# Dense groups cut into contraction steps over the mixers' slots, earlier rounding of weights, and 16 modulation units moved beside layer 0's feed-forward

## The reference, cut to what matters

```python
for layer in range(2):
    mod_l = adaln_params(c, w_mod[layer], b_mod[layer])        # silu(c) @ w_mod + b_mod, six vectors of 1024
    mod_c = adaln_params(c_ctx, w_mod[layer], b_mod[layer])
    p_l = modulate(x,   norm1_g, mod_l[0], mod_l[1]) @ w_in    # modulate: rmsnorm(x, g) * (1 + scale) + shift
    p_c = modulate(ctx, norm1_g, mod_c[0], mod_c[1]) @ w_in
    a = diff_attention(p[0:3]); b = hgrn2_mixer(p[3:8]); n = neighbourhood_attention(p[8:11]); w = window_gqa(p[11:14])
    x = x + mod_l[2] * (concat(a, b, n, w) @ w_out)
    x = x + mod_l[5] * (square(relu(modulate(x, norm2_g, mod_l[3], mod_l[4]) @ w_ff1)) @ w_ff2)
    # layer 0 does the last two lines for ctx too; layer 1 for x alone
```

## Time and profile before

| what | value |
|---|---|
| median of 3 runs | 2527.3 us (2523.86, 2527.3, 2529.58) |
| profiled execution, its own time | 2523.21 us |
| its span, first to last instruction | 2521.4 us |
| TensorE busy | 2078.6 us (82%) |
| VectorE, ScalarE, GpSimd busy | 1159.5, 766.8, 610.0 us |
| mean granted TensorE clock | 0.908 |
| loads of 1 MB of `w_ff` and `w_mod`, issue to landing, median | 5.3 us |
| GpSimd's `wlo` of one unit (L637), mean | 4.6 us |
| chain that ended last | TensorE 67%, VectorE 17%, ScalarE 9% |

### The profile page before, as it was taken

The page is one execution under the profiler, slowest core; times in us unless marked ns, Lnnn a source line. Parts: engine busy times, 40 slices in busy tenths (PEclk is TensorE's granted clock), DMA queues, the critical chain, the costliest instruction groups (busy, mean ns, idle before and its releaser), DMA issues.

```text
span 2521.4 us, 29860 instructions
## 1 busy us (share of the span) xinstructions
PE 2078.6 (82%) x12484; PEld 1705.4 (68%) x12484; DVE 1159.5 (46%) x1782; ACT 766.8 (30%) x1225; POOL 610.0 (24%) x263
## 2 busy tenths in 40 slices
PE   5779786687775698999999997879688639899998
PEld 3667564466664586888888885658477536688887
DVE  2544536555499715222221316454685884522322
ACT  2522222223333325222221315232344432522321
POOL 0121010001166122222222221301001552344432
PEclk9889797778898798999999998989799778999999
DMA  7312020323165011122112212111001011232231
GB/s 261 59 51 84 1 67 1 101 88 80 42 204 193 5 51 49 52 67 67 57 62 67 68 50 39 55 33 34 17 18 51 0 34 51 67 100 88 96 100 67
DMA packets 178918, 168.86 MB, mean 67 GB/s; under 512 B 29200, under 2 KB 176096, under 8 KB 178656
## 3 DMA queue, kind: packets, MB, share of 16 engines
q1 hardware_dynamic: 176704, 161.18, 20.9%
q10 hardware_dynamic: 2080, 5.77, 0.8%
HBM read 159.07 MB, written 2.10 MB: 64 GB/s over the span
## 4 chain that ended last, share of the span: by engine, by line
PE 67%; DVE 17%; ACT 9%; issue 4%; POOL 2%; DMA 1%; ACTq 0%; SPq 0%; DVEq 0%; POOLq 0%
PE gp L691 53%; PE sp L823 3%; PE gp L858 2%; ACT DA_p L1184 2%; POOL HGx_kd L613 2%; PE sp L734 1%; PE tp L838 1%; ACT nt L1097 1%; PE sp L814 1%; PE gp L712 1%; DVE small L1578 1%; DVE sp L1453 1%; PE sp L921 1%; DVE sp L1452 1%; DMA raw<-in_w_mod 1%
## 5 line engine op out<-in xcount | busy, mean ns | idle before, releaser
L637 POOL TENSOR_TENSOR wlo<-raw,whi 128x2048 fp32r<-128x2048 f32 x98 | 452.4, 4617 | 1684.3 <-ACT whi L1079 1684.1
L691 PE MATMUL gp<-xhi,whi 128*128 128x512 f32 (+1 forms) x1584 | 584.1, 369 | 114.5 <-DVE xlo L1473 53.0
L691 PE MATMUL gp<-xlo,whi 128*128 128x512 f32 (+1 forms) x1584 | 570.8, 360 | 0.0
L691 PE MATMUL gp<-xhi,wlo 128*128 128x512 f32 (+1 forms) x1584 | 569.3, 359 | 0.0
L691 PEld LDWEIGHTS gp<-xhi,whi 128*128 128x128 f32 x1584 | 312.1, 197 | 170.2 <-issue 55.8
L691 PEld LDWEIGHTS gp<-xlo,whi 128*128 128x128 f32 x1584 | 311.7, 197 | 43.0 <-issue 1.7
L691 PEld LDWEIGHTS gp<-xhi,wlo 128*128 128x128 f32 x1584 | 310.8, 196 | 43.2
L1079 ACT ACTIVATE whi<-raw 128x2048 fp32r<-128x2048 f32 x98 | 186.8, 1908 | 426.3 <-PE gp L691 425.2
L1833 DVE SCALAR_TENSOR_TENSOR xT<-gp,mods,xT 128x512 f32<-128x512 f32 x120 | 78.6, 662 | 475.9 <-PE gp L691 475.9
L691 PE MATMUL gp<-hhi,whi 128*128 128x512 f32 (+1 forms) x768 | 273.7, 356 | 9.3 <-ACT frel L1393 6.3
L691 PE MATMUL gp<-hlo,whi 128*128 128x512 f32 (+1 forms) x768 | 272.1, 354 | 0.0
(11 more groups left out here) (304 smaller groups left out, 2864.3 us busy)
## 6 DMA issues: line engine op xcount, KB each, us to landing
raw<-in_w_ff SPq DMA_DIRECT2D x64, 1024.0 KB, 5.3
raw<-in_w_mod SPq DMA_DIRECT2D x48, 1024.0 KB, 5.3
raw<-in_w_in SPq DMA_DIRECT2D x20, 1024.0 KB, 5.1
raw<-in_w_in SPq DMA_DIRECT2D x24, 256.0 KB, 4.3
raw<-in_w_out SPq DMA_DIRECT2D x8, 768.0 KB, 4.7
bias<-e SPq DMA_DIRECT2D x96, 32.0 KB
xin<-in_x ACTq DMA_DIRECT2D x1, 2048.0 KB, 9.2
raw<-in_w_out SPq DMA_DIRECT2D x16, 128.0 KB, 4.7
```

Source lines behind the costliest of these rows:

```text
L637: nc.gpsimd.tensor_tensor(wlo[:, s % 2, :, :], raw[:, index[splits[s]] % 2, :, :], whi[:, s % 2, :, :].bitcast(F32), ALU.subtract).then_in ...
L691: mm = pe.matmul(out, lhs, rhs, start=(i == 0 and j == 0), stop=(i == KT - 1 and j == 2))
```

## The change: what it does

1. The plan of the slots (`fill_plan`) spreads a mixer's work by its weight (a step of a 512-token group counts 2, of any other group 1, a row 4/8) evenly over its slots, and may cut a dense group between two contraction steps. The bank stays occupied from one slot to the next.
2. Modulation units in layer 0: none in NA and SW, 14 in DA, 10 in HG, and the last 16 (layer 1's j = 2 to 5) beside layer 0's feed-forward: a row after one unit, its turn after the next, so that each second feed-forward unit has a modulation unit behind it in the load order.
3. `after_unit` emits a rounding once the `whi` slot is free and, if the raw slot was a modulation unit's, that one's row has been passed; the condition on unit i-2 for dense units is gone.
4. On VectorE in the attention mixers, all groups that end in a slot but the last are read ahead of `finish(n + 1)`; the last stays behind it. `ENDS` lists the groups that end in each slot.
5. The norm at the start of a layer waits for that layer's j = 0 and 1 alone.

```diff
+    counts = {("NA", 0): 0, ("SW", 0): 0, ("DA", 0): 14, ("HG", 0): 10, ("NA", 1): 0, ("SW", 1): 0, ("DA", 1): 0, ("HG", 1): 0}
...
+            work = []
+            put = 0
+            for i, (u, c) in enumerate(chunks):
+                work.append((u, c, 2 if c[0] != "tok" and c[1] == 0 else 1))
+                closing = i + 1 < len(chunks) and chunks[i + 1][0] != u
+                while not closing and put < len(units) * (i + 1) // len(chunks):
+                    work.append((units[put], "row", 3))
+                    put += 1
+            work += [(u, "row", 3) for u in units[put:]]
+            total = sum(8 * w if c != "row" else 4 for _, c, w in work)
+            slots = [[] for _ in range(n + 1)]
+            s, done, turn = 0, 0, None
+            for u, c, w in work:
+                if c == "row":
+                    if turn:
+                        slots[s].append(turn)
+                    slots[s].append((u, "row", 0, KT))
+                    turn = (u, "turn", 0, KT)
+                    done += 4
+                    s = min(max(s + 1, done * n // total), n)
+                    continue
+                if turn:
+                    slots[s].append(turn)
+                    turn = None
+                k0 = 0
+                for k in range(KT):
+                    done += w
+                    if done * n >= (s + 1) * total and k < KT - 1:
+                        slots[s].append((u, c, k0, k + 1))
+                        k0 = k + 1
+                        s = min(s + 1, n - 1)
+                slots[s].append((u, c, k0, KT))
...
+            spots = [(0, q, kind, j) for q in range(4) for kind in ("ff1", "ff2") for j in range(4)]
+            for i, u in enumerate(mods):
+                plan["FF"][spots[2 * i]].append((u, "row"))
+                plan["FF"][spots[2 * i + 1]].append((u, "turn"))
...
+ENDS = {key: [[(u, c) for u, c, _, b in slot if b == KT] for slot in slots] for key, slots in FILL.items()}
...
-            def dense(u, *cs, ready=None):
+            def dense(u, *cs, ready=None, part=range(KT)):
...
-                for i, k in enumerate(MIX_ORDER if u[0] == "out" else range(KT)):
+                for i in part:
+                    k = MIX_ORDER[i] if u[0] == "out" else i
...
             def after_unit(u):
-                reached[0] = max(reached[0], index[u])
+                reached[0] = max(reached[0], last_group(u))
...
-                    if index[v] - 2 > reached[0]:
+                    before = units[index[v] - 2]
+                    if before[0] == "mod" and last_group(before) > reached[0]:
                         return
-                    before = units[index[v] - 2] if index[v] >= 2 else None
-                    if before and before[0] == "mod" and last_group(before) > last_group(u):
-                        return
-                    if s >= 2 and last_group(splits[s - 2]) > last_group(u):
+                    if s >= 2 and last_group(splits[s - 2]) > reached[0]:
                         return
...
+                    fill(ENDS[m, l][n][:-1])
                     finish(n + 1)
-                    fill(FILL[m, l][n])
+                    fill(ENDS[m, l][n][-1:])
                     output(n)
...
+                        for w, c in beside(l, q, "ff1", j):
+                            modulation(w, c)
...
+                        for w, c in beside(l, q, "ff2", j):
+                            modulation(w, c)
```

More of the change, by code:

```diff
@@ L139, in fill_plan @@
         tiles = 6 if l < DEPTH - 1 else 4
[L140 to L155, removed]
-            plan[m, l] = slots
@@ L157, in fill_plan @@
-    assert not mods
+        for m, names, n in (("NA", ("SWq", "SWkv"), 2 * tiles), ("SW", ("DAq", "DAk", "DAv"), 2 * tiles),
+                            ("DA", ("HGq", "HGi"), 4 * tiles), ("HG", (), 6 * tiles)):
+            chunks = [(("prj", l, name), c) for name in names for c in chunks_of(("prj", l, name))]
+            units = [mods.pop(0) for _ in range(counts[m, l])]
+            work = []
[30 more added lines that the diff above has]
+                slots[s].append((u, c, k0, KT))
+                if 10 * done * n >= (10 * s + 6) * total:
+                    s = min(s + 1, n - 1)
+            if turn:
+                slots[s].append(turn)
+            plan[m, l] = slots
@@ L179, in dense_order @@
         for m in ("NA", "SW", "DA"):
-            groups.extend((u, c, one) for slot in FILL[m, l] for u, c in slot)
+            groups.extend((u, c, one) for slot in FILL[m, l] for u, c, a, _ in slot if a == 0)
         for n in ("HGf0", "HGf1", "HGg"):
             whole(("prj", l, n))
-        groups.extend((u, c, both) for slot in FILL["HG", l] for u, c in slot)
+        groups.extend((u, c, both) for slot in FILL["HG", l] for u, c, a, _ in slot if a == 0)
         for j in range(4):
@@ L189, in dense_order @@
                     whole((kind, l, q, j))
+                    groups.extend((u, c, both) for u, c in beside(l, q, kind, j))
     return groups
@@ L721, in fill @@
             def fill(slot):
-                for u, c in slot:
+                for u, c, a, b in slot:
                     if u[0] == "mod":
@@ L1283, in hgrn @@
                         if idx >= 4:
-                            fill(FILL["HG", l][idx - 4])
+                            fill(ENDS["HG", l][idx - 4])
                         idx += 1
                 read_out(ntile - 1)
-                for slot in FILL["HG", l][-5:]:
+                for slot in ENDS["HG", l][-5:]:
                     fill(slot)
@@ L1366, in _ @@
                     if before:
-                        fill(FILL[before, l][-2])
-                        fill(FILL[before, l][-1])
+                        fill(ENDS[before, l][-2])
+                        fill(ENDS[before, l][-1])
                     attention(m, l)
@@ L1918, in _ @@
                              .then_inc(ls(l, "h_split"), 1)
+                        fill(beside(l, q, "ff1", j))
                     for j in range(4):
                         add_back(("ff2", l, q, j), 5, l)
+                        fill(beside(l, q, "ff2", j))
                     wait_read(dve, ("ff2", l, q, 3))
```

36 lines of the change are left out of this document (23 added, 13 removed).

## The result

The changed kernel takes 2553.1 us (median of 4 runs, 2543.1 to 2557.2) against 2528.1 for the kernel before in the same comparison (2523.9 to 2529.6): ratio 1.0096, 95% interval 1.0072 to 1.012. It is slower by 25 us, where +7 was forecast. The profiled execution took 2552.55 us (span 2550.7).

| stretch | before | after | change | forecast |
|---|---|---|---|---|
| start to the first NA transposes | 161.6 | 169.5 | +8.0 | +0.9 |
| NA slots, layer 0 | 83.3 | 67.0 | -16.3 | -14.9 |
| SW slots, layer 0 | 105.7 | 88.3 | -17.4 | -15 |
| end of SW's slots to DA's first | 47.3 | 50.9 | +3.6 | 0 |
| DA slots, layer 0 | 176.5 | 157.6 | -18.9 | -16 |

The account below looks back on a forecast made before the run. TensorE was taken to bound NA, SW and feed-forward, VectorE HG, and waits for VectorE's reads to idle TensorE in layer 0's DA. Terms -14 - 15 - 16 + 11.5 - 2 + 35 + 7.5 = +7 gave 2534 us, range 2509 to 2556.

Parts of the forecast that it names:

- its rivals: Whole kernel: DA's clock comes back, 2516, chance 0.28; end of DA covered, 2522, 0.13; feed-forward loses clock, about 2570, 0.08.
- three signs of being wrong: DA's slots under 150 us, feed-forward under 575, or HGf0's first read no later after DA's last slot than before.
- The end of DA: Behind layer 0's DA: HGf0's and HGf1's loads wait for the last modulation rows, roundings precede the squares; +11.5 us.
- Feed-forward, +35: Layer 0's feed-forward: 16 units 24.5, four turn reads +4.2, slow stretches +5, landing waits +1, banks +0.8; +35 us.
- SWkv's rounding ... +0.9: Ahead of layer 0's NA: SWkv's 1.9 us rounding now precedes the copies of NA's values; +0.9 us (0 to 1.9).
- twelve units fewer: -3.5: Layer 0's HG: each unit costs VectorE at most 0.42 + 0.15 us, reads partly overlap; -3.5 us.
- Layer 1, +7.5: Layer 1: cut groups bring late reads, DA +3.2, HGf1's rounding +1.3, NA +3, SW 0; +7.5 us (0 to 13).
- DA, -16: Layer 0's DA slots: shorter waits, early waits, units, pieces, clock and longer loop sum to -16 us (0 to -35).
- 21.6 less 9: Layer 0's DA: earlier reads of turns save 21.6 us of waits, new early waits in ten slots cost 9.
- 20 us that a slot by slot sum leaves unexplained: Layer 0's DA: 20 us unexplained by a slot by slot sum at full clock, of which 6 are taken back.
- The rival that the clock comes back: Layer 0's DA: clock rises from 0.77 to 0.92 to 0.95, DA gives 34 instead of 16, total 2516; chance 0.28.
- The clock term: Layer 0's DA: fewer long waits return clock, -6 us; by the Trainium skill's rule it would be near 0.

Follow-up runs that it names:

- run 4: Changed kernel, with GpSimd's low part of SWq waiting for VectorE's four NA low parts and SWkv rounded behind the copies of NA's values: 2543.9 us, ratio 1.0067.
- run 2: Changed kernel, with layer 0's DA units placed so the last two rows stand in slots 20 and 21: 2542.6 us, ratio 1.0059.
- run 11: Changed kernel with 12 DA and 28 HG units, early read before pieces, both edits ahead of NA, DA's last roundings behind its norm: 2458.1 us, ratio 0.972.
- run 1: Changed kernel, with the 16 modulation units beside layer 0's feed-forward put back into layer 0's HG slots (26 there): 2506.8 us, ratio 0.9917.
- run 3: Changed kernel, with VectorE reading a slot's last group ahead of finish too where a further piece follows: 2517.6 us, ratio 0.9969.
- run 6: Changed kernel, with every read of a slot's groups behind finish, as in the kernel before: 2605.5 us, ratio 1.0314.
- run 8: Changed kernel with the kernel before's unit counts (4 NA, 2 SW, 12 DA, 22 HG, none beside the feed-forward): 2504.0 us, ratio 0.9907.
- run 5: Changed kernel with feed-forward units back in HG, DA's last rows earlier, early read before pieces, and two edits ahead of NA: 2471.9 us, ratio 0.9777.
- run 7: Kernel before, with one edit alone: all groups in a slot but the last are read ahead of finish: 2482.5 us, ratio 0.9823.
- run 9: The kernel with all four edits (2471.9 us), with 12 units in DA, 28 in HG, and DA's roundings two slots later on ScalarE: 2469.1 us, ratio 0.9769.

## Why the forecast came out as it did

**Right in direction and in most of its chain of causes, too low by 18 to 22 us.** The 2553 us measured lie inside the range given (2509 to 2556), but outside the forecast's own (2522 to 2546): the range held by the room that it left for its rivals, none of which came true. "Slower" stood at 0.49, so the direction was half luck. Five stretches were 4 to 7 us longer than written, and the largest error the other way was 2.9. None of the three signs of being wrong showed: the DA slots took 157.6 us (150.7 in run 4, at the edge of the 150 named), the feed-forward 578.2, the first read of HGf0 came 14 us later.

No wait for `mods` is left in NA and SW, none for `wlo` in SW; four waits of 3.9 us in DA and three long ones in layer 1's DA (two for HG_v, together 7.8, one of 4.1 for HG_q) are where the argument put them; two roundings stand ahead of the squares and end 15.2 us behind the last transposes, where 13.4 was written. The end of DA was sized at +11.5 and measured +14.1, and runs 2 and 11 show 10 us of it caused by the squares behind roundings whose loads the last rows gate.

**Feed-forward, +35 against +39.7.** Idle time rose from 4.9 to 13.3 us; 7.1 of the 13.3 are the four turn reads. The clock's share was smaller than the +5 written: two slow stretches, not three. TensorE's busy time rose by 31.3 (run 1's 533.58 to 564.88) where 24.5 of instructions and 3.4 of clock were due; the last 3.4 stay open. The forecast missed one thing beside it: the units shift GpSimd's low parts against VectorE's squares of 128x512, which take 1144 ns in the mean instead of 861. Whether that cost TensorE anything is not shown.

**Start of NA, +0.9 against +8.0.** The step "SWkv's rounding ... +0.9" counted what the rounding does on its own engine. Some 4 us were the collision, which no instruction of the change makes and which several runs of the same program text escape.

**HG, -2 against +3.1.** The step "twelve units fewer: -3.5" failed. With 10 units the levels took 102.6 to 107.7 us in six profiles at clocks of 0.80 to 0.88, with 22 101.2 to 104.6 at 0.90 to 0.94, with 26 104.7 and 104.4 at 0.95 and 0.96, with 28 106.7 and 109.5 at 0.98 and 0.95. VectorE's saved reads are real (95.5 to 92.4 us busy), but its idle time grew by twice as much (5.7 to 11.9 us). Of that growth 2.7 us are waits for a row that TensorE had not finished, shown in the section on the result. The lower clock, with TensorE's scores as a link of the chain, may be the rest: that is read from these rows, no run changed the clock alone, and the 28 units at 0.98 and 0.95 show that the clock does not settle it. The cause stays open.

**Behind SW, 0 against +3.6; the same between layer 1's mixers.** The forecast stopped at the last transposes. The new plan fills the last slot with more groups (two of 3.1 us where one stood), and the product with the values, which the next head norms wait for, is behind them. No run tested this.

**Layer 1, +7.5 against +12.4.** Again a sum of parts that were off both ways. Between its mixers it lost 3.7 and 3.6 us, in its DA slots 7.3 where 3.2 was written, at their end 2.5 for 1.3; NA's slots, written at +3, and SW's, at 0, gave back 2.0 and 2.2.

**DA, -16 against -18.9: the right sum from wrong parts.** The read order is worth 44 us on the new plan and 32 on the old, not 21.6 less 9, and the plan costs 25 or 13, where "two more units +3.1" and "pieces of 2 to 3 us: -4" were written. The "20 us that a slot by slot sum leaves unexplained", of which 6 were taken back, stand in no row. The rival that the clock comes back is the part that was underrated. In the four slots of run 3 a wait taken away returned one and a half times its length. Over the runs less idle time goes with a higher clock, but loosely: idle 58.4, 44.7, 33.8, 23.3, 19.6 and 15.6 us at clocks of 0.71, 0.77, 0.84, 0.89, 0.91 and 0.88 (run 6, before, after, runs 3, 8 and 11), yet 29.6 at 0.90, 22.7 at 0.85 and 19.8 at 0.82 in runs 5, 7 and 9. What else sets it is open. The rival did not decide here: with the four late reads in place the clock was 0.84 to 0.87, below the 0.88 from which it was to count. The clock term itself was written as -6. Time at half clock, worked out from 0.77 of 176.5 us and 0.84 of 157.6, went from 81 to 50 us; with TensorE busy three quarters of it, that is an estimated 12 us. The rule cited from the Trainium skill ("TensorE: Matmul & The Clock Gate", section "A second HAM failure mode: psum-queue depth-cycling") agrees in kind for the kernel before and run 6, more idle between groups and more half clock; the 0 that was read from it for this term does not, and run 9 had less idle time than the changed kernel at a lower clock.

## What to carry to other kernels

Work moved to where an engine is 99% busy costs its whole length, and where it left may give nothing back; look for idle time on the engine that pays, stage by stage. When one wait has two causes (an order of reads, a plan), try each alone: here a one-line reordering gave 45 us by itself, and the plan and the moved units around it took back more than that. A freed buffer is not a landed load: ScalarE, told to round it at once, stood still in front of it for 8.14 us at the end of DA, 4.24 in slot 9 and 5.75 in run 5. One profile of a stage whose clock moves is one sample: the same DA slots took 151 to 158 us.

## What the hardware showed that was not expected

A VectorE operation with two SBUF operands (or the scaling by a column) that starts while GpSimd subtracts 128x2048 ends 0.15 to 0.8 us behind GpSimd's end: 5.24 us for 1.38, 3.28 for 0.34, 4.72 for 0.69 (the squares in the feed-forward); those that read PSUM do not wait. It goes the other way too: where VectorE's third low part of NA started first, in runs 2, 7 and 8, GpSimd's subtraction took 5.25 us instead of 4.55. The Trainium skill has this in "SBUF — State Buffer", section "SBUF: two separate sides": the pair of ports that VectorE and GpSimd share is locked for a whole instruction. The trace agrees, run 11's rows above all.
